# Fourteen of the sixteen merge gate tiles computed in pairs by seven block products, placed behind the convolution's up-projection

## The reference

```python
h = rmsnorm(x, g_mix[l]) * (1.0 + sc_a) + sh_a
z = h @ w_in[l] + b_in[l]
(cb, cc, cu, q, kc, vc, k_s, v_s, k_w, v_w, nsa_g, merge_g) = jnp.split(z, split_at, axis=-1)
y_conv = short_conv_mixer(cb, cc, cu, conv_w[l]) @ w_up_conv[l]
...
g_conv, g_attn = jnp.split(jax.nn.sigmoid(merge_g), 2, axis=-1)
mixed = (g_conv * y_conv + g_attn * y_attn) @ w_o[l]
x = x + ga_a * mixed
```

## Time and profile before

| | |
|---|---|
| time, median of 3 runs | 3276.86 us (3276.48 to 3279.43) |
| the profiled execution: its time / its span | 3278.76 us / 3277.0 us |
| PE busy in the span | 3171.2 us (97%) |
| DVE / ACT / POOL busy | 1855.7 / 972.1 / 1544.1 us |
| mean granted clock of PE, of full speed | 0.988 |
| moved by DMA | 264.16 MB, 81 GB/s |

### The profile page before, as it was taken

One profiled execution on the slowest core, in us unless ns is written; L12 is line 12 of the kernel. 1 busy time (PEld: TensorE's weight loads), 2 busy tenths in 40 slices (PEclk: granted clock), 3 DMA queues, 4 the chain that ended last, 5 costly groups with the idle time before them and its releaser, 6 DMA issues.

```text
span 3277.0 us, 40421 instructions
## 1 busy us (share of the span) xinstructions
PE 3171.2 (97%) x15183; PEld 2589.9 (79%) x15213; DVE 1855.7 (57%) x2507; ACT 972.1 (30%) x1771; POOL 1544.1 (47%) x1727
## 2 busy tenths in 40 slices
PE   8999999998899999999999999999989999999998
PEld 6888887676688888888778888877767888888887
DVE  7533246887536666555565332478864545555555
ACT  2100114666212222222220001257661222222233
POOL 3433332233454656666744333323334656666665
PEclk8999999999899999999999999999999999999999
DMA  7333621000522222111243345200005211111112
GB/s 262 119 116 129 187 77 39 1 1 1 199 62 68 78 78 78 52 52 52 78 144 99 119 141 174 59 20 1 1 14 199 65 52 52 52 52 52 52 52 97
DMA packets 294440, 264.16 MB, mean 81 GB/s; under 512 B 10347, under 2 KB 274791, under 8 KB 293736
## 3 DMA queue, kind: packets, MB, share of 16 engines
q1 hardware_dynamic: 279410, 207.66, 21.2%
q10 hardware_dynamic: 14838, 53.94, 4.4%
HBM read 223.81 MB, written 30.41 MB: 78 GB/s over the span
## 4 chain that ended last, share of the span: by engine, by line
PE 87%; DVE 8%; issue 2%; ACT 2%; POOL 1%; DMA 0%; ACTq 0%; DVEq 0%; POOLq 0%; SPq 0%
PE lin L1187 56%; PE lin L1536 16%; PE aux L1427 2%; DVE pTL L2119 2%; PE pv L1443 2%; PE pv L1444 1%; DVE negm L2095 1%; PE lin L1403 1%; PE lin L1404 1%; PE pv L1292 1%; ACT pTH L1754 1%; PE lin L1369 1%; PE lin L1237 1%; PE lin L1238 1%; PE lin L1239 1%
## 5 line engine op out<-in xcount | busy, mean ns | idle before, releaser
L1158 POOL TENSOR_SCALAR unit<-wraw 128x512 fp32r<-128x512 f32 x396 | 324.9, 820 | 1002.4 <-PE lin L1187 687.0
L1187 PE MATMUL lin<-hH,unit 128*128 128x512 f32 x2272 | 715.0, 391 | 1.2 <-POOL wlo L1160 1.2
L1187 PE MATMUL lin<-hL,unit 128*128 128x512 f32 x2272 | 710.9, 389 | 0.0
L1187 PE MATMUL lin<-hH,wlo 128*128 128x512 f32 x2272 | 710.4, 389 | 0.0
L1160 POOL TENSOR_TENSOR wlo<-wraw,unit 128x512 fp32r<-128x512 f32 x396 | 562.6, 1421 | 33.0
L1187 PEld LDWEIGHTS lin<-hH,wlo 128*128 128x128 f32 x2272 | 426.5, 188 | 89.8
L1187 PEld LDWEIGHTS lin<-hL,unit 128*128 128x128 f32 x2272 | 426.5, 188 | 89.1 <-issue 0.2
L1187 PEld LDWEIGHTS lin<-hH,unit 128*128 128x128 f32 x2272 | 423.4, 188 | 88.8 <-issue 2.8
L1536 PE MATMUL lin<-fH,unit 128*128 128x512 f32 x1568 | 486.8, 390 | 4.2 <-DVE xT L2255 3.5
L2255 DVE SCALAR_TENSOR_TENSOR xT<-lin,adac,xT 128x512 f32<-128x512 f32 x448 | 328.9, 748 | 182.5 <-PE lin L1536 177.8
L1104 POOL TENSOR_SCALAR prob<-prob,fac 128x640 f32<-128x640 f32 (+7 forms) x256 | 184.2, 719 | 441.6 <-DVE fac L2089 423.7
(11 more groups left out here) (282 smaller groups left out, 4461.5 us busy)
## 6 DMA issues: line engine op xcount, KB each, us to landing
wraw<-in_w_ff SPq DMA_DIRECT2D x136, 512.0 KB, 3.9
wraw<-in_w_ada SPq DMA_DIRECT2D x80, 512.0 KB, 3.7
wraw<-in_w_in SPq DMA_DIRECT2D x78, 512.0 KB, 4.9
wraw<-in_w_o SPq DMA_DIRECT2D x24, 512.0 KB, 3.9
adar<-in_w_ada SPq DMA_DIRECT2D x16, 512.0 KB, 11.8
x_keep<-xT ACTq DMA_DIRECT2D x4, 2048.0 KB, 8.6
mix_keep<-tmp ACTq DMA_DIRECT2D x16, 512.0 KB, 3.1
gate_keep<-ropes ACTq DMA_DIRECT2D x16, 512.0 KB, 6.7
```

The source lines that it names most:

```text
L1158: pool.tensor_scalar(high, raw, 1.0, 1.0, ALU.mult, ALU.mult).then_inc(w_hi, 1)
L1187: mm = pe.matmul(lin[c % 2][:, hf], w, m(k, hf), start=first, stop=last)
```

## The change

The stage is put in another order, and 14 of its 16 gate tiles are computed another way.

- **Order.** `cc`, `cu`, `cb` four times as before, with three ada tiles per round in the first two rounds and six in the last two; then `ga0` with two ada tiles, the eight `uc` with three ada tiles behind each two, `ga1`, and then seven pairs of gate tiles: `ga2` to `ga7`, `gc0` to `gc7`. Then `kc`, `vc`, `q0`.
- **Seven products.** A pair of tiles (`mate` and `wide`) has the blocks a11, a12 (first tile, upper and lower half of its rows) and a21, a22. POOL makes four sums of 128x512 in `wsum` and seven low parts, ACT the seven high parts. `hH`/`hL` are summed too, once a layer: T1 = H12 - H11, T2 = H22 - T1, T3 = H22 - H12, T4 = H21 - T2, each in two pieces of 128x1024 (`hf_piece`, two or three `TENSOR_TENSOR` on DVE), a high part on ACT (`hf_high`) and a low part on DVE (`hf_low`). PE runs `wide_products`, 7 x 12 = 84 matmuls a pair in place of 96.
- **Evictions.** The four result blocks of a pair take the four halves of the two `lin` buffers. ACT copies four products out into `fbuf` (`cbuf`), DVE adds four times PSUM and `fbuf` (128x512), ACT applies four sigmoids of 128x512.
- **The up-projection** is no longer multiplied with its gate when it is evicted: ACT copies `uc` to `tmp` and stores it; it is read back later (`fetch_y`), multiplied on DVE with the gate and stored again.
- **Places.** A sixth raw slot `xraw` takes every fourth tile of the pairs; high and low forms use two of eight units each, so four forms are alive at a time. `ga1` is put into slot 4 in both layers. In layer 0 this slot held the ada tile that is fourth from the end (the last of `ADA_UP[2]`), in layer 1 the one that is next to last (the second of the three behind the last `uc`).
- **Compression loads.** All 16 are issued behind `q0`'s load, and the first waits until all forms of the last pair are made and its fourth product is done. The tables for rope are fetched after the last product, in both layers.
- Some semaphores are shared by both layers, with counts to match.

```diff
+ADA_CONV = ((0, 2, 1), (1, 1, 1), (2, 2, 2), (2, 2, 2))
+ADA_GATE, ADA_UP = (2, 0), (3, 3, 3, 3)
+GATES = [("ga", i) for i in range(2, KC)] + [("gc", i) for i in range(KC)]
+WIDE = len(GATES) // 2
...
+        dense("w_in", 0, O_MG + D, [("ga", 0)], ADA_GATE[0])
         for i in range(0, KC, 2):
-            dense("w_in", 0, O_MG + P * i, [("gc", i)], 1)
-            dense("w_in", 0, O_MG + P * (i + 1), [("gc", i + 1)], 1)
-            dense("w_up_conv", 0, P * i, [("uc", i), ("uc", i + 1)], 1)
-        for i in range(KC):
-            dense("w_in", 0, O_MG + D + P * i, [("ga", i)], 1)
+            dense("w_up_conv", 0, P * i, [("uc", i), ("uc", i + 1)], ADA_UP[i // 2])
+        dense("w_in", 0, O_MG + D + P, [("ga", 1)], ADA_GATE[1])
+        for q in range(WIDE):
+            for kind, (g, i) in zip(("mate", "wide"), GATES[2 * q:2 * q + 2]):
+                tiles.append((kind, layer, "w_in", 0, O_MG + D * (g == "ga") + P * i, KC, ("gates", q)))
...
+            while mode == "pairs" and at % RAW not in RAW_FF or name == ("ua", 0) and at % RAW != RAW - 2 or name == ("ga", 1) and at % RAW != RAW - 1:
+                at += 1
...
                 if kv == t == 0:
-                    sp.wait_ge(lin_done, CHUNK[layer, ("uc", KC - 1)] + 1)
+                    sp.wait_ge(form_lo, PRODUCTS * pair0)
+                    sp.wait_ge(prod_done, PRODUCTS * pair0 - 3)
...
+                def wide_products(q):
...
+                    for i in range(PRODUCTS):
+                        if q == 0 and i in HF_READY:
+                            pe.wait_ge(hf_lo, 8 * layer + HF_READY[i])
+                        pe.wait_ge(form_lo, PRODUCTS * p + i + 1)
+                        if q == 0 and i in (0, 2):
+                            c = CHUNK[layer, ("ga", 1)] - (i == 2)
+                            pe.wait_ge(lin_free[c % 2], c // 2 + 1)
...
+                        for k in range(4):
+                            for w, m in ((wh, mh), (wh, ml), (wl, mh)):
+                                mm = pe.matmul(bank, w[:, k * P:(k + 1) * P], m[:, k, :], start=begins and w is wh and m is mh and k == 0,
...
+                dense(("ga", 0), H, L)
+                for _ in range(ADA_GATE[0]):
                     ada(next(nxt))
+                pe.wait_ge(cv_lo, v0 + 4)
+                for i in range(KC):
+                    dense(("uc", i), lambda k, hf: cvH[:, k, hf], lambda k, hf: cvL[:, k, hf])
+                    if i % 2:
+                        for _ in range(ADA_UP[i // 2]):
+                            ada(next(nxt))
+                dense(("ga", 1), H, L)
...
+                for i in range(KC):
+                    if i >= 2:
+                        act.wait_ge(mix_out[i % 2], 16 * KC * layer + 16 * (i // 2))
+                    done(act, ("uc", i))
+                    act.activation(tmp[:, i % 2, :], slot(("uc", i))[:, :], ACT.Copy).then_inc(free_sem(("uc", i)), 1)
+                    freed(act, ("uc", i))
+                    act.dma_start(mix_keep[i], tmp[:, i % 2, :]).then_inc(mix_out[i % 2], 16)
+                    if i % 2:
+                        hf_high(2 + i // 2)
+                wide_high(0, 0)
+                wide_high(0, 1)
+                hf_high(6)
+                hf_high(7)
+                gate(1)
+                wide_high(0, 2)
+                wide_high(0, 3)
...
+                ada_tiles_of(ADA_GATE[0] + ADA_UP[0])
+                hf_piece(2)
+                hf_low(0)
+                ada_tiles_of(ADA_UP[1])
+                hf_piece(3)
+                hf_low(1)
+                ada_tiles_of(ADA_UP[2])
+                hf_piece(4)
+                ada_tiles_of(ADA_UP[3])
+                hf_piece(5)
+                hf_low(4)
+                ada_tiles_of(ADA_GATE[1])
+                hf_low(5)
+                done(dve, ("uc", KC - 1))
+                hf_piece(6)
+                hf_low(2)
+                hf_piece(7)
+                hf_low(3)
+                hf_low(6)
+                hf_low(7)
```

432 lines of the change are left out of this document (326 added, 106 removed).

## The result

| | before | after |
|---|---|---|
| time, median | 3278.5 us (8 runs, 3276.3 to 3280.7) | 3289.0 us (8 runs, 3283.4 to 3295.4) |
| after / before | | 1.0031, 95% interval 1.0021 to 1.0041 |
| the profiled execution: time / span | 3278.76 / 3277.0 us | 3295.41 / 3293.7 us |
| PE busy | 3171.2 us | 3147.6 us |
| mean granted clock | 0.988 | 0.982 |

The change makes the kernel 10.5 us slower; 3267 us, 10 us faster, had been forecast, and the time lies outside the range. Which of its terms is smaller in the other executions no trace of this kernel shows.

The account below looks back on a forecast made before the run. PE, busy 3171.2 of 3277.0 us, was taken as the bound. -38.4 saved, +13.8, +1.8 and +12.5 of waits and clock gave -10.3 from 3276.9: 3267 us, range 3246 to 3281.

Parts of the forecast that it names:

- The saving and the pairs: Seven pairs in two layers: 12 matmuls less a pair, 38.4 us saved; POOL's cover in the pairs 4.8 us, no cost.
- The way in: Ada tiles and DVE's sums of h before the pairs: first product 13.8 us late in layer 0, 12.5 in layer 1.
- I take 2.0 for six of the seven: DVE's last seven instructions up to T4, six beside POOL at 2.0 us each: 13.3 us.
- the first rival's case: Strict alternation of POOL and DVE on SBUF operands: 1.8 to 3.3 us more per layer, 3270 to 3273 us; chance 0.2.
- Little cover is left, but no wait: Rounds with six ada tiles: DVE has 30 us of work in 33.6, so PE does not wait.
- The half clock: PE at the 1.2 GHz level for eight matmuls behind a wait: 1.8 us lost, added once in layer 0.
- One bound: Bounds on the waits, from DVE never slowed to slowed in every instruction: 23 to 37 us, time 3260 to 3276.
- The compression loads: ... Hidden: 16 loads behind the pairs land before `compress(0)`, 44 us after the pairs end; `blk` had 15.8 us cover, no wait.
- the rotation of `kc` now queues behind three tile loads, some 3 us: Ahead of the compression product: `kc`'s rotation delayed some 3 us by three tile loads, hidden by cover.
- the waits eat the gain: Rival: another 5 to 15 us from rounds with little cover or a second low clock, 3272 to 3282 us; chance 0.13.

Follow-up runs that it names:

- e14: The changed kernel with POOL's first sum of the first pair made to wait for all eight DVE sums of h, both layers: 3291.9 us, one run.
- e1: The changed kernel with the eight `cmp_v` loads behind q3's load and `kc`'s rotation, not behind q0's load: 3283.2 us, ratio 1.0017.
- e4: The kernel before with its 16 compression loads in one block behind q0's load, nothing else changed: 3277.3 us, ratio 1.0001.
- e13: Changed kernel, first pair reordered, `ga1` early in layer 1, `cmp_v` behind rotation, ada tile moved, POOL padded, layer 1 pair forms two units on: 3252.2 us.
- e9: Changed kernel, first pair reordered, `ga1` loaded early in layer 1, `cmp_v` behind `kc`'s rotation, 32 met waits in POOL's stream at layer 1's start: 3262.4 us.

## Why the prediction was wrong

**The saving and the pairs: right.** A pair takes 19.05 us, 12 matmuls of 0.228 less than two tiles; once the first product has started PE waits nowhere inside the pairs of either layer, and POOL is not their bound.

**The way in: right in mechanism, under-sized.** 13.8 and 12.5 us had been forecast, plus 1.8 once for the clock: 28.1. Measured, with the clock behind them: 1.3 + 14.0 + 2.9 = 18.2 us in layer 0 and 1.2 + 9.0 + 1.8 + 4.3 = 16.3 in layer 1, together 34.5. The 14.0 for 13.8 is luck in part: `ga1` ended at 257.9 and not 254.6, the first product came at 271.8 and not 268.4. Of its pieces, DVE was done with the last piece of T3 2.5 us later than worked out (255.2, not 252.7), and "I take 2.0 for six of the seven" should have been the row's 2.2: 14.4 us in place of 13.3. That is the first rival's case, and e14 shows that the turns are strict (1.22 us alone, 2.32 beside POOL). It bears out the rule of the Trainium skill, "SBUF — State Buffer", section "SBUF: two separate sides", that one of the two holds the ports for a whole instruction. The case had been given a chance of only 0.2 because of a median of 1226 ns, which was of instructions that POOL had left alone. "Little cover is left, but no wait" was wrong by 1.3 and 1.2 us. The half clock, counted as 1.8 us once, came in both layers, 7.2 us in all. One bound was also added up wrong: 23 us of waits give 3261.5 us, not 3260.

**"The compression loads: ... Hidden": the step that failed.** The working counted bytes up to `compress(0)` and put "the rotation of `kc` now queues behind three tile loads, some 3 us". The rotation also stands behind 16 loads whose issues take 26.4 us, and was 14.3 us late, 9.6 of them by the block (e1); with its slower landing, `blk` was 18.4 us late against 15.8 us of cover. No price had been put on issuing, the landing had been read where two loads go at a time, and what else starts there after the change, the rope tables and the last y, was not added. It cost 11.3 us in both layers in the trace of after. e1 gets back 6 in the median; the 4.5 us of layer 1 are larger in after's trace than in any other kernel with the block, so they may belong to that execution alone. e4 shows that the block alone would have been hidden, as the step said.

**Not in the sum at all:** 2.3 us before `kc` in layer 1, from the unit that the planner gives to `kc`'s high part there (e13), and 4.4 us in the output projection of layer 1, which came with the 0.29 us (e9, e14); what makes the 0.29 us stays open.

The forecast's sum was -10.3. Trace to trace, +6.4 from the way in, +11.3 from the compression product, +2.3 and +4.4 make it +14.1 of the measured 16.7; the rest is 1.0 unassigned in the two stages and 1.6 from attention and the end. The last rival, "the waits eat the gain", priced 5 to 15 us more than the forecast's and 0.13; it is the nearest to what came, and it too had left out the loads.
